# Sums of squares for the first mixer's head norm: from VectorE's reductions to ScalarE's activations

## The reference

```python
s = jnp.einsum('bqhmd,bkhmd->bhmqk', q_blk, k).astype(F32) * scale + bias[None, :, None]
p = jax.nn.softmax(s, axis=-1)
a = (p[:, :, 0] - lam * p[:, :, 1]).astype(v.dtype)
return jnp.einsum('bhqk,bkhe->bqhe', a, v)
...
o = rms_norm(o, subln_g) * (1.0 - lam_init)     # over the 128 columns of each head
...
return jnp.concatenate([o, om], axis=-1) @ w_out   # om: attention of 4 heads to a memory of 256 rows
```

## Time and profile before

| | us |
|---|---|
| time, median of 3 runs | 1804.37 |
| lowest, highest run | 1803.39, 1805.27 |
| profiled execution, span from first to last instruction | 1799.5 |
| profiled execution, its own total | not recorded |
| PE busy in the span | 1754.1 (97%) |
| DVE busy | 1413.2 (79%) |
| ACT busy | 1115.2 (62%) |
| POOL busy | 124.3 (7%) |
| mean granted TensorE clock | 0.996 of full |

### The profile page before, as it was taken

The page is one execution under the profiler, slowest core; times in us unless marked ns, Lnnn a source line. Parts: engine busy times, 40 slices in busy tenths (PEclk is TensorE's granted clock), DMA queues, the critical chain, the costliest instruction groups (busy, mean ns, idle before and its releaser), DMA issues.

```text
span 1799.5 us, 22262 instructions
## 1 busy us (share of the span) xinstructions
PE 1754.1 (97%) x8373; PEld 1437.5 (80%) x8383; DVE 1413.2 (79%) x1213; ACT 1115.2 (62%) x1026; POOL 124.3 (7%) x159
## 2 busy tenths in 40 slices
PE   8989999999999999999999999999999989999998
PEld 6867888788768888888888888888888868778886
DVE  5567788767778888889888888888889877476556
ACT  6664444452567777777777777777777756543333
POOL 3030111022030000000000000000001010000000
PEclk9999999999999999999999999999999999999999
DMA  9637899653269999999999999999999985535550
GB/s 319 212 125 251 302 326 323 233 178 129 94 241 382 384 380 382 378 380 382 378 384 382 379 383 379 387 368 378 380 372 386 393 296 178 151 122 194 187 187 24
DMA packets 237420, 525.95 MB, mean 292 GB/s; under 512 B 17066, under 2 KB 40810, under 8 KB 237184
## 3 DMA queue, kind: packets, MB, share of 16 engines
q1 hardware_dynamic: 223376, 477.23, 73.5%
q0 software_dynamic: 13936, 47.32, 7.8%
HBM read 513.95 MB, written 10.53 MB: 291 GB/s over the span
## 4 chain that ended last, share of the span: by engine, by line
PE 91%; DVE 4%; ACT 2%; DMA 1%; issue 1%; DVEq 0%; SPq 0%; ACTq 0%
PE bank L2885 28%; PE bank L2886 27%; PE bank L2893 27%; PE bank L3350 1%; DVE w_lo L1704 1%; PE bank L3037 1%; PE bank L2941 1%; ACT w_hi L1063 1%; DMA raw<-in_moe_w_down 1%; PE bank L2999 1%; DMA raw<-in_a_w_mem_kv 1%; PE bank L2948 0%; PE bank L3709 0%; PE bank L2966 0%; PE bank L3384 0%
## 5 line engine op out<-in xcount | busy, mean ns | idle before, releaser
L1704 DVE TENSOR_TENSOR w_lo<-raw,w_hi 128x2048 fp32r<-128x2048 f32 x453 | 1040.6, 2300 | 211.8 <-ACT w_hi L1063 201.1
L1063 ACT ACTIVATE w_hi<-raw 128x2048 fp32r<-128x2048 f32 x453 | 867.5, 1916 | 468.9 <-PE bank L2886 340.0
L2885 PE MATMUL bank<-w_hi,slot_hi 128*128 128x512 f32 x896 | 355.2, 396 | 0.9 <-DVE slot_lo L2420 0.9
L2886 PE MATMUL bank<-w_hi,slot_lo 128*128 128x512 f32 x896 | 349.5, 390 | 0.0
L2885 PE MATMUL bank<-w_hi,hT_hi 128*128 128x512 f32 (+1 forms) x704 | 277.6, 395 | 7.3 <-DVE hT_lo L1769 2.5
L2886 PE MATMUL bank<-w_hi,hT_lo 128*128 128x512 f32 (+1 forms) x704 | 272.8, 388 | 0.0
L2893 PE MATMUL bank<-w_lo,slot_hi 128*128 128x512 f32 x896 | 240.7, 390 | 1.7 <-DVE w_lo L1704 1.7
L2893 PEld LDWEIGHTS bank<-w_lo,slot_hi 128*128 128x128 f32 x896 | 167.7, 188 | 39.3 <-DVE w_lo L1704 4.0
L2885 PEld LDWEIGHTS bank<-w_hi,slot_hi 128*128 128x128 f32 x896 | 168.4, 188 | 34.3 <-DVE slot_lo L2420 1.1
L2886 PEld LDWEIGHTS bank<-w_hi,slot_lo 128*128 128x128 f32 x896 | 168.4, 188 | 33.3
L2893 PE MATMUL bank<-w_lo,hT_hi 128*128 128x512 f32 (+1 forms) x704 | 173.4, 388 | 0.0
(11 more groups left out here) (432 smaller groups left out, 1434.2 us busy)
## 6 DMA issues: line engine op xcount, KB each, us to landing
raw<-in_moe_w_gate_up SPq DMA_DIRECT2D x448, 512.0 KB, 5.8
raw<-in_moe_w_down SPq DMA_DIRECT2D x224, 512.0 KB, 5.8
raw<-in_w_ff SPq DMA_DIRECT2D x64, 512.0 KB, 4.4
work<-in_w_ada POOLq DMA_DIRECT2D x48, 512.0 KB, 5.6
raw<-in_dense_w_gate_up SPq DMA_DIRECT2D x44, 512.0 KB, 5.4
raw<-in_b_w_in SPq DMA_DIRECT2D x24, 512.0 KB, 5.1
raw<-in_w_in SPq DMA_DIRECT2D x24, 512.0 KB, 5.0
raw<-in_dense_w_down SPq DMA_DIRECT2D x22, 512.0 KB, 4.7
```

Of the source, the lines that this page charges most:

```text
L1063: act.activation(w_hi[:, g % SPLIT, 0:n], raw[:, g % RING, 0:n], ACT.Copy).then_inc(R.hi, 1)
L1704: dve.tensor_tensor(w_lo[:, g % SPLIT, 0:n], raw[:, g % RING, 0:n], f32(w_hi[:, g % SPLIT, 0:n]), ALU.subtract).then_inc(R.lo, 1)
L2885: pe.matmul(out_, hi, w_hi[:, s, c:c + w], start=(start and n == 0), stop=False, skip_group_check=True)
L2886: mm = pe.matmul(out_, lo, w_hi[:, s, c:c + w], start=False, stop=False, skip_group_check=True)
```

## The change

DVE no longer computes the sums of squares: `value_out` ends with the copy, which now raises "out". ACT gets `head_squares(n)`: it waits for "out" of head n and runs, for each of the two tiles, a Square activation of the copied 128x128 block in `mix` with an accumulated sum into the same column of `headsq`; the second raises "squared". In ACT's round n it stands for head n-1 between exponentials n+1 and turned_out n, and for head 5 between exponentials 7 and `load_sqrt`. POOL's gain multiply waits for "squared" in place of "out", and DVE waits for "squared" of head 5 ahead of the variances. The scratch for the squares is twice as wide, so that the two tiles have their own.

```diff
--- before.py
+++ after.py
@@ -428,7 +428,7 @@
         def diff_bias(i):
             return work[:, 4096 + i * SEEN:4096 + (i + 1) * SEEN]
 
-        diff_squares = work[:, 9472:9600]
+        diff_squares = work[:, 9472:9728]
 
         def diff_item(i):
             k = i % 2
@@ -926,7 +926,7 @@
             if have("diff"):
                 pool.wait_ge(gain_in[0], 16)
                 for i in range(DA_HEADS):
-                    pool.wait_ge(*at(f"diff{i}", "out"))
+                    pool.wait_ge(*at(f"diff{i}", "squared"))
                     o = mix[:, :, i * P:(i + 1) * P]
                     pool.tensor_tensor(o, o, gain[:, 0, 0:P].unsqueeze(1).broadcast_to([P, TILES, P]), ALU.mult)\
                         .then_inc(S("diff", "weighted", i), 1)
@@ -1184,6 +1184,14 @@
                 else:
                     c = act.activation(it.turned, bank[4 + it.n % 2][:, 0:SEEN], ACT.Copy)
                 c.then_inc(S(it.tag, "copied"), 1)
+
+            def head_squares(it):
+
+                act.wait_ge(*at(it.tag, "out"))
+                for t in range(TILES):
+                    q = act.activation(diff_squares[:, t * P:(t + 1) * P], mix[:, t, it.first:it.first + P], ACT.Square,
+                                       accum_out=headsq[:, 2 * it.n + t:2 * it.n + t + 1])
+                q.then_inc(S(it.tag, "squared"), 1)
 
             def head_norm(tag):
                 act.wait_ge(*at(tag, "head variance"))
@@ -1275,10 +1283,12 @@
                 exponentials(a_items[1], None)
                 for n in range(1, DA_HEADS):
                     exponentials(a_items[n + 1], at(f"diff{DA_HEADS - 2}", "turned") if n + 1 == DA_HEADS else None)
+                    head_squares(a_items[n - 1])
                     turned_out(a_items[n], at(f"diff{n - 2}", "values") if n >= 2 else None)
                     if n == 3:
                         split_hi(ring, G["a_out"], 0)
                 exponentials(a_items[DA_HEADS + 1], None)
+                head_squares(a_items[DA_HEADS - 1])
                 load_sqrt()
                 turned_out(a_items[DA_HEADS], at(f"diff{DA_HEADS - 1}", "scores"))
                 head_norm("diff")
@@ -1821,12 +1831,6 @@
                 if it.kind == "diff":
                     dve.wait_ge(*at(it.tag, "values"))
                     dve.tensor_copy(mix[:, :, it.first:it.first + P], o.rearrange("p (t d) -> p t d", t=TILES)).then_inc(S(), 1)
-                    dve.wait_ge(*S.last())
-                    for t in range(TILES):
-                        q = dve.tensor_tensor_reduce(diff_squares, o[:, t * P:(t + 1) * P], mix[:, t, it.first:it.first + P], 1.0, 0.0,
-                                                     ALU.mult, ALU.add, headsq[:, 2 * it.n + t:2 * it.n + t + 1])
-                        q.then_inc(S(), 1)
-                        dve.wait_ge(*S.last())
                 else:
                     r = sums[:, it.n, :]
                     dve.wait_ge(*at(it.tag, "exp"))
@@ -2090,6 +2094,7 @@
 
 
                 f = (1.0 - LAM_INIT) ** 2
+                dve.wait_ge(*at(f"diff{DA_HEADS - 1}", "squared"))
                 s0 = sums[:, 0:DA_HEADS, 0:2]
                 sq = headsq[:, 0:2 * DA_HEADS].rearrange("p (i t) -> p i t", t=TILES)
                 dve.scalar_tensor_tensor(out=s0, in0=s0, scalar=EPS / f, in1=s0, op0=ALU.mult, op1=ALU.mult).then_inc(S(), 1)
```

## The result

The changed kernel takes 1807.68 us (median of 20 runs, 1804.45 to 1810.08) against 1804.12 (20 runs, 1801.46 to 1805.73): ratio 1.0020, interval 1.0014 to 1.0026, or +3.6 us (2.5 to 4.7). Forecast were 1807.3 and a range of 1804.9 to 1808.9; the loss lies just on the 0.2% that I had called measurable.

A forecast was written before the change was run, and what follows sets the result against it. The prediction took the chain of waits, 91% on PE, as the bound, with ACT limiting the changed head rounds. Tail +1.3 and clock +1.6 gave +2.9 us on the 1804.37 median: 1807.3 us, range 1804.9 to 1808.9.

The forecast's parts named there:

- A head's pace: First mixer's head rounds: one turn, copy to copy on DVE, falls from 4.07 us to 2.88 us.
- What DVE could save: DVE in the head rounds: up to 1.19 us per head, 5.9 us over five, of which 0.9 arrives.
- ACT as the bound from the split on: Head rounds after two heads: from the weight split at 113.46 us ACT never waits; its work eats DVE's saving.
- The squares: Squares added on ACT: 0.30 us each, 0.60 a head, 3.6 us for twelve (3.5 to 4.6).
- The low bound: Estimate from below for one 128x128 Square on ACT: 0.29 us, from a 512-wide Square less 384 elements.
- No table load: ACT between heads: Square needs no other table than exponentials; the rival, +14 us and 1818, had chance 0.02.
- The tie for the port: Head 5: POOL's multiply and DVE's second mixing operation tie for the SBUF port; if POOL wins, 0.7 us more.
- The tail: After the rounds: squares(5) ahead of ACT's table load delay it +0.96 us; range to +2.3, taken as +1.3.
- The clock: PE from the value products on: a 2.9 to 3.2 us gap brings a fall towards 1.2 GHz, +1.6 us.
- Faster: Rival for the head rounds: ACT bounds less, five turns keep DVE's saving; -3.9 us, 1800.5; chance 0.05.
- copy 5: ACT's copy of head 5's turned probabilities: forecast at 121.22 us; more than 2.0 us before 122.1 decides for "Faster".
- clock-stays case: Rival at the value products: PE stays at 2.4 GHz, +0.96 to +2.3 us, about 1805.7; chance 0.27.

The follow-up runs named there:

- split_early: Changed kernel with the output product's weight split moved out of ACT's head rounds to behind head 0's exponentials; ratio 1.0002 against the kernel before.
- idle_added: Changed kernel with idle matmuls on zeros in three PE gaps: before head 5's transposes, before its copied probabilities, before value products 6; ratio 1.0015 against the kernel before.
- split_early_before: Kernel before, squares still on DVE, with the output product's weight split moved early on ACT; ratio 1.0000 against the kernel before.
- rebuilt: Changed kernel with early weight split, squares behind the next head's probability copy, head 5's behind table load and memory head 6's copy; ratio 1.0009 against the kernel before.
- rebuilt_idle: rebuilt plus idle matmuls on zeros on PE, six ahead of value products 6 and two behind; ratio 0.9989 against the kernel before.

## Why the prediction came out right, point by point

- **A head's pace**: 2.88 us forecast, 2.84 and 2.99 measured. What DVE could save, 5.9 us, was read too high: the 4.07 is the longest turn, and DVE's small sum operation stands beside GpSimd's multiply in four heads (0.65, 0.59, 0.58 and 0.58 us against 0.22), so some 5.3; the forecast does not hang on it, since ACT lets only 0.9 through. ACT as the bound from the split on: forecast to 0.01 us (split at 113.46 + 0.98 = 114.44, measured 114.43; reciprocal 5 at 118.11, measured 118.12). split_early shows that it was the split that used up ACT's room.
- **The squares**: 0.30 us each; median 298 ns, two starts 0.31 and 0.29 apart. The low bound was right, 0.38 too high, and so was the 0.41 estimated from the Trainium skill ("ScalarE: Activation LUTs", Rules for kernel authors): its 0.3 us is for an ACTIVATE whose bias is a pointer operand, and the added Square is given none. The exponentials of the same size, which have one, took 0.39 us.
- **No table load** for Square: none is in ACT's timeline between the heads.
- **The tie for the port**: GpSimd won in head 5, +0.47, where I had allowed 0.7. The Trainium skill's rule ("SBUF — State Buffer", Who interferes with whom) holds both ways: DVE's mixing took 1.22 us with GpSimd's multiply beside it, and the multiply for head 1, which started second (111.26, behind a mixing operation from 110.95), took 1.03 instead of the 0.72 of the earlier trace rows.
- **The tail**: the wait of squares(5) for DVE's last copy ahead of the table load. Forecast +0.96, with the measured 0.47 of the tie +1.4, taken as +1.3; with the clock up (idle_added) it is +1.33. Moved, the loss halves (1.0010), and the 0.9 us that its trace still shows is the moved tail's own; alone, it makes the whole loss (1.0028). This is the cause.
- **The clock**, the term that was mis-sized: "I expect it: +1.6", one fall behind the gap ahead of value products 6. Both profiles of the changed kernel have two: the first from 120 or 122 us costs 1.5 between the idle matmuls and DVE's last copy (126.89 - 122.68 = 4.21 against 2.69); the second lasts 7 us, not some 3. Together 4.5 us at the low parts of the first, 2.9 more than I gave. Two errors nearly met, and that is luck: the clock cost more in these executions, and the kernel before loses clock in its own, which I put at nothing; so the medians moved less (+3.6, and 1.0028 in the second timing) than the profiled executions (+5.7 and +7.0 in "rest"). The granted clocks give the size. In 89 executions of the kernel before they run from 0.992 to 0.998 with a median of 0.994, where its first profile had 0.996; the changed kernel has a median of 0.992 in both timings, and its profiles 0.992 and 0.990. Those of the 89 at 0.992 took 1806.0 us in median, those at 0.996 1801.7, some 1.0 us for 0.001. So between the medians the clock makes some 2 us, an estimate, which with 1.3 of waiting comes near the 3.6. Where the executions that were not profiled lose it stays open.
- **The reading behind that term was wrong**: I took gaps of 2.4 us and more as what brings a fall. The clock fell with a longest gap of 1.07 us (split_early_before) and 1.33 (rebuilt), and held in before with 1.06, at the same work on PE. All these falls came in a stretch where PE does short transposes and 64-column products between waits, but that stretch is in the kernel before too, so what decides stays open. What the runs show is the remedy: with idle matmuls in the gaps the clock stayed at 1.00 (idle_added, rebuilt_idle; one profile each). The Trainium skill ("TensorE: Matmul & The Clock Gate", Part 1) ties the clock to how busy PE has been, and these two agree with that.
- The rival "Faster" fell on the point named: copy 5 came 0.4 us earlier, not 2. In rebuilt it came 3.8 earlier, and the gain was still lost to the clock.
- A slip: the low end of the clock-stays case less 0.5 is 1804.8 (1804.37 + 0.96 - 0.5), not 1804.9; nothing hangs on it.

## What to carry to other kernels

Moving work off a busy engine moves its place in another engine's order: ask of each new wait what stands behind it. Here one wait for the last head, ahead of a table load, cost more than five heads' savings gave. And count TensorE's clock with any change in a stretch where the engines wait for each other: a gain of 3 us was worth nothing until a few idle matmuls kept the clock up.

## What the runs showed of the hardware

- A spell at 1.2 GHz in a stretch of small fp32 matmuls cost 2.9 us (35.3 against 32.4 at the low parts, same waits), where the clock's shortfall in one amid 512-column products comes to 1.7, an estimate from the earlier trace rows. The difference is its length: the clock was low over 130 to 138 us in the first, over 172 to 176 in the second. Sixteen products of 64 columns took 3.52 us against 1.90, 1.9 times as long; 512-column products start 0.43 us apart in a spell and 0.23 outside one, as much.
- Such a spell can begin with no wait over 1.1 us.
- A 128x128 Square with an accumulated sum: 298 ns, its read-out of 187 ns overlapped so that the next starts 0.29 to 0.31 us behind.
- The start of an execution (up to the first head's reciprocal) varied from 103.3 to 106.4 us over twelve profiles, and the clock goes with it: 103.3 to 103.7 in the four whose granted clock stayed at 1.00 there, 104.7 to 106.4 in the eight with a spell between 12 and 20 us.
